# Head norms of three attention stages: squares in two float32r parts made by GpSimd, two single passes on TensorE

## The chip, the cores and the metric

The kernel runs on one core of a Trainium2 chip. The metric is the device time of one execution in microseconds, as the median of several runs. TensorE is the matrix engine, VectorE, ScalarE and GpSimd work element by element, SyncE issues the DMAs.

## The reference

Three transformer blocks over 512 tokens of width 1024, batch 1. The first has differential attention (4 heads with two maps each) beside a pooling mixer, the second sliding-window attention with sinks, the third a state-space scan (SSD, 16 heads) beside forgetting attention (16 heads); a gated feed-forward layer with a convolution follows each. In all three attentions queries and keys are normalised head by head (64 values each) before the scores:

```python
def rms_norm(x, g):
    xf = x.astype(jnp.float32)
    y = xf * lax.rsqrt(jnp.mean(xf * xf, axis=-1, keepdims=True) + EPS)
    return (y * g.astype(jnp.float32)).astype(x.dtype)

# differential attention: q, k of (B, S, 4 heads, 2, 64)
q = rms_norm(q.reshape(B, S, A_HEADS, 2, A_HEAD_DIM), q_g)
k = rms_norm(k.reshape(B, S, A_HEADS, 2, A_HEAD_DIM), k_g)
# sliding window: 16 query heads on 2 key heads; the sink is one more logit
m = jnp.maximum(jnp.max(s, axis=-1, keepdims=True), sink)
p = jnp.exp(s - m)
denom = jnp.sum(p, axis=-1, keepdims=True) + jnp.exp(sink - m)
# forgetting attention: 16 heads
qh = rms_norm_2(heads(q), q_norm_w)
kh = rms_norm_2(heads(k), k_norm_w)
```

## The kernel before

Activations lie transposed: the features on 128 partitions, the 512 tokens along a row, so that one chunk is 128x512 and holds two heads of 64. Weights come by DMA as slabs of up to 128x2048, ScalarE rounds each to float32r (w_hi) and VectorE subtracts (w_lo); a projection is three passes for each 128x128 block, w_hi with x_hi, w_hi with x_lo and w_lo with x_hi.

All engines have their own program, written out by hand in one order, and meet only by semaphores. The stages are A (differential attention), F0, C (sliding window), F1, S with the state-space scan and, at its end and after it, X (forgetting attention), and F2. Within A, C, the scan and X the projection matmuls are woven (L1178) between the small steps of the attention, in quotas that are fixed in advance, so that TensorE has work while the other engines do the softmax. In these stages step g is one block of 128 queries of two heads: scores (L862 in A, L1221 in C, L1095 in X), a woven part, the transposes of the step before (L870, L1231, L1104), then a norm job, and the values of two steps before (L881, L1246, L1117). VectorE's order in a step is finish (reciprocal of the sums and scaling of the exponentials: L1984 and L1986 in A, L2141 in C, L2503 in X), maxima (L1972, L2128, L2492), then evacuations, weight splits (L2082, 128x1024 halves) and the scaling of the next queries and keys (L1957, L2106, L2462). In A it also does the pool groups, a scan and subtractions (L2555 to L2561).

A norm job has five steps. GpSimd squares a chunk of 128x512 (L635 in A, 8 jobs; L653 in C, 10; L676 in X, 16) into a float32 tile, sq_q or sq_k by turns. TensorE multiplies with pair_ones, a float32 128x128 matrix with two blocks of 64x64 ones, which sums the squares of each head and spreads the sum over its 64 partitions (L812, L1210, L1067). ScalarE makes the inverse root by logarithm and exponential (L1419 and L1423, L1536 and L1540, L1712 and L1716), and VectorE scales the chunk. A square may overwrite its tile when TensorE has read it, which is the wait for d_stat, c_stat or f_stat. In X the queries, keys and values of a head pair come back from the scratch memory by three DMAs, for which f_in counts, and the first two jobs also wait for the last heads of the scan (y_done), whose seg and c_grow tiles lie where sq_q and sq_k do. GpSimd further multiplies C by the growing decay in the scan (L666), makes low parts of outputs (L642, L682) and sums squares for the token norms (L621).

In C the maximum of a step takes the sink in from neg_sink, and the sink's logit stands in column 256 of each probability tile (sink_columns, L2117), so that the exponential, written in place over 257 columns, adds it to the sum. There are two pairs of such tiles, used by steps in turn.

## Time and profile before

| | us |
|---|---|
| median of 3 runs | 1938.52 |
| lowest and highest | 1936.71 to 1938.80 |
| the profiled execution, its own time | 1936.25 |
| its span in the profile | 1934.4 |
| TensorE matmul busy | 1899.7 |
| VectorE busy | 1188.0 |
| ScalarE busy | 794.5 |
| GpSimd busy | 138.0 |

The span is from the first to the last instruction of the profiled execution; its own time has 1.9 us more around it. Busy times are sums of the durations of instructions; a matmul's end is modelled, so matmuls overlap in the record, and what one costs is read from start to start. In the timelines a row is one instruction or a few of the same kind: start, time from the first start to the last end, engine, line, operation and tiles, and in brackets how long the engine had stood idle before it and what released it. PE is TensorE, PEld its loading of weights, DVE VectorE, ACT ScalarE, POOL GpSimd.

By stage, A is from 0 to about 180 us, C from 565 to 740, the scan from 1190 to 1365 and X from there to 1570; the feed-forward layers lie between.

### The profile page before, as it was taken

What the parts mean: (1) busy time and instruction counts of PE and PEld (TensorE: products, weight loads), DVE (VectorE), ACT (ScalarE), POOL (GpSimd) and SP (SyncE); (2) the same over time, 40 slices, a digit from 0 to 9 for tenths busy, and PEclk for the clock granted to TensorE, in tenths of its full rate; (3) what the DMA queues carried; (4) which work ended last, traced back from release to release, by engine and by line L of the source; (5) the groups of instructions that cost most, each with busy time, mean ns of one, the idle gap of its engine ahead of it and who ended that gap; (6) DMA issues with size and microseconds to landing.
All of it is one profiled execution on the core that took longest, in us unless ns stands there. A gap on an engine that the chain in (4) does not pass through costs nothing.

```text
span 1934.4 us, 24585 instructions
## 1 busy us (share of the span) xinstructions
PE 1899.7 (98%) x9034; PEld 1504.6 (78%) x9034; DVE 1188.0 (61%) x1852; ACT 794.5 (41%) x1237; POOL 138.0 (7%) x102
## 2 busy tenths in 40 slices
PE   8999999999999999999999999999999999999999
PEld 6767888888786668888887887878666688888887
DVE  5686677356546756764476488674555667743762
ACT  4355443234435654332244433332466544422431
POOL 2011100000011001000000101111201020000000
PEclk9999999999999999999999999999999999999999
DMA  5111322322231112223322332344423122223222
GB/s 212 66 44 67 107 88 87 109 90 98 76 117 66 45 44 87 87 92 103 109 87 69 115 106 93 131 133 158 150 100 124 56 87 88 97 98 109 87 76 98
DMA packets 38304, 186.51 MB, mean 96 GB/s; under 512 B 4384, under 2 KB 4768, under 8 KB 23376
## 3 DMA queue, kind: packets, MB, share of 16 engines
q1 hardware_dynamic: 37936, 185.22, 28.3%
q8 instruction: 49, 0.80, 0.2%
q14 instruction: 31, 0.25, 0.0%
q10 hardware_dynamic: 288, 0.23, 0.0%
HBM read 176.95 MB, written 8.49 MB: 96 GB/s over the span
## 4 chain that ended last, share of the span: by engine, by line
PE 87%; DVE 7%; ACT 3%; issue 2%; DMA 0%; SPq 0%; POOL 0%; ACTq 0%; DVEq 0%; POOLq 0%
PE banks L706 54%; PE banks L1178 20%; PE banks L756 3%; DVE w_lo L1835 1%; DVE w_lo L2082 1%; PE banks L1117 1%; PE banks L1095 1%; ACT w_hi L1326 1%; PE banks L1104 1%; PE banks L1221 1%; ACT w_hi L1526 1%; DVE tmp L2211 1%; PE banks L1067 1%; PE banks L1246 1%; PE banks L1191 1%
## 5 line engine op out<-in xcount | busy, mean ns | idle before, releaser
L706 PE MATMUL banks<-xn_hi,w_hi 128*128 128x512 f32 x1240 | 486.4, 392 | 8.5 <-DVE w_lo L2584 6.0
L706 PE MATMUL banks<-xn_hi,w_lo 128*128 128x512 f32 x1240 | 483.4, 390 | 0.0
L706 PE MATMUL banks<-xn_lo,w_hi 128*128 128x512 f32 x1240 | 478.0, 390 | 0.0
L1835 DVE TENSOR_TENSOR w_lo<-raw,w_hi 128x2048 fp32r<-128x2048 f32 (+3 forms) x135 | 279.3, 2069 | 69.0 <-ACT w_hi L1326 68.5
L1326 ACT ACTIVATE w_hi<-raw 128x2048 fp32r<-128x2048 f32 (+3 forms) x135 | 229.9, 1703 | 178.0 <-PE banks L706 148.4
L706 PEld LDWEIGHTS banks<-xn_hi,w_hi 128*128 128x128 f32 x1240 | 233.4, 188 | 59.6 <-DMA con<-consts 6.0
L706 PEld LDWEIGHTS banks<-xn_lo,w_hi 128*128 128x128 f32 x1240 | 233.4, 188 | 49.8 <-issue 1.4
L706 PEld LDWEIGHTS banks<-xn_hi,w_lo 128*128 128x128 f32 x1240 | 233.4, 188 | 48.5
L1385 ACT ACTIVATE tmp<-scaled_h,par 128x512 f32<-128x512 f32 x132 | 100.5, 809 | 349.9 <-DVE scaled_h L1880 349.9
L1880 DVE TENSOR_TENSOR scaled_h<-banks,token_rs 128x512 f32<-128x512 f32 x132 | 85.0, 686 | 185.9 <-PE banks L706 165.6
L1178 PE MATMUL banks<-xn_hi,w_hi 128*128 128x512 f32 x408 | 166.1, 407 | 3.3 <-DVE w_lo L2082 3.3
L1178 PE MATMUL banks<-xn_hi,w_lo 128*128 128x512 f32 x408 | 163.1, 400 | 0.0
L1178 PE MATMUL banks<-xn_lo,w_hi 128*128 128x512 f32 x408 | 162.8, 399 | 0.0
L706 PE MATMUL banks<-hid_hi,w_hi 128*128 128x512 f32 x396 | 154.3, 390 | 1.5 <-DVE w_lo L1835 1.5
L706 PE MATMUL banks<-hid_hi,w_lo 128*128 128x512 f32 x396 | 154.1, 389 | 0.0
L706 PE MATMUL banks<-hid_lo,w_hi 128*128 128x512 f32 x396 | 154.0, 389 | 0.0
L1853 DVE TENSOR_TENSOR x<-banks,x 128x512 f32<-128x512 f32 (+1 forms) x48 | 33.2, 691 | 156.6 <-PE banks L706 137.8
L1888 DVE SCALAR_TENSOR_TENSOR tmp<-scaled_h,par,tmp 128x511 f32<-128x511 f32 x132 | 98.7, 748 | 35.4 <-ACT tmp L1385 35.4
L621 POOL TENSOR_TENSOR sq<-sq 128x512 f32<-128x512 f32 x38 | 55.9, 1470 | 873.1 <-ACT sq L1332 855.9
L2082 DVE TENSOR_TENSOR w_lo<-raw,w_hi 128x1024 fp32r<-128x1024 f32 x62 | 79.7, 1288 | 52.1 <-ACT w_hi L1526 52.1
L1892 DVE SCALAR_TENSOR_TENSOR tmp<-scaled_h,par,tmp 128x510 f32<-128x510 f32 x132 | 99.0, 750 | 14.5 <-DVE tmp L1888 12.4
L1178 PEld LDWEIGHTS banks<-xn_hi,w_hi 128*128 128x128 f32 x408 | 76.6, 188 | 30.8 <-issue 10.5
(270 smaller groups left out, 2605.2 us busy)
## 6 DMA issues: line engine op xcount, KB each, us to landing
raw<-weights SPq DMA_DIRECT2D x116, 1024.0 KB, 4.9
raw<-weights SPq DMA_DIRECT2D x24, 768.0 KB, 4.4
raw<-weights SPq DMA_DIRECT2D x24, 640.0 KB, 3.9
big<-scratch SPq DMA_DIRECT2D x40, 256.0 KB, 5.0
att<-scratch SPq DMA_DIRECT2D x16, 256.0 KB, 4.6
scratch<-stage SPq DMA_DIRECT2D x12, 256.0 KB, 4.2
scratch<-con SPq DMA_DIRECT2D x12, 256.0 KB, 2.0
out<-x SPq DMA_DIRECT2D x4, 512.0 KB, 4.0
```

The lines of the kernel that those rows point to most:

```text
L621: pool.tensor_tensor(chunk(sq, 0), chunk(sq, 0), chunk(sq, c), ALU.add).then_inc(sq_summed, 1)
L706: return pe.matmul(psum[:, 2 * p + m, :], w[:, at_:at_ + P], x_part(k), start=start, stop=stop)
L756: return pe.matmul(psum[:, 2 * (s % 2), :], w[:, at_:at_ + P], x_part(k), start=(k == 0 and t == 0), stop=(k == k_n - 1 and t == 2))
L1178: ins = pe.matmul(c_bank(u), w[:, at_:at_ + P], x_part(k), start=(k == 0 and t == 0), stop=(k == k_n - 1 and t == 2))
L1326: act.activation(w_hi[:, sl], raw[:, sl], ACT.Identity).then_inc(hi_done, 1)
L1385: act.activation(chunk(tmp, 2 * j + m), chunk(scaled_h, 2 * j + m), ACT.Identity, bias=pcol(conv_b, c), scale=pcol(conv, 3 * c + 2)).then_ ...
L1835: dve.tensor_tensor(w_lo[:, sl], raw[:, sl], w_hi[:, sl].bitcast(F32), ALU.subtract).then_inc(lo_done, 1)
L1853: last = dve.tensor_tensor(chunk(x, c), psum[:, 2 * ((a + j) % 2) + m, :], chunk(x, c), ALU.add)
L1880: dve.tensor_tensor(chunk(scaled_h, 2 * j + m), psum[:, 2 * ((a + j) % 2) + m, :], token_rs[:, :], ALU.mult).then_inc(h_scaled, 1)
L1888: me.mark(dve.scalar_tensor_tensor(out=chunk(tmp, t, 1), in0=bank[:, 0:T - 1], scalar=pcol(conv, 3 * c + 1), in1=chunk(tmp, t, 1), op0=ALU ...
L1892: dve.scalar_tensor_tensor(out=chunk(tmp, t, 2), in0=bank[:, 0:T - 2], scalar=pcol(conv, 3 * c), in1=chunk(tmp, t, 2), op0=ALU.mult, op1=A ...
L2082: ins = dve.tensor_tensor(w_lo[:, sl], raw[:, sl], w_hi[:, sl].bitcast(F32), ALU.subtract)
```

## The change

Squares and ones become float32r. A job on GpSimd is now `squares_of`: square into the float32 tile `squared`, copy that to a float32r tile (the high part), and subtract the high part from the square into a second float32r tile (the low part). Each step waits for the one before through a semaphore of GpSimd's own, pool_self, and the last for its own count. The wait for TensorE's reading stands ahead of the copy now, no longer ahead of the square. TensorE multiplies both parts with pair_ones in two accumulating products. pair_ones is a float32r tile, which VectorE copies once from the constants at the start of A (pair_ready); TensorE waits for it ahead of its first job.

The parts lie by turns in tn 1 and more 1 (jobs 0, 2, ...) and in more 2 and stage (jobs 1, 3, ...; in X more 0 instead of stage). The first job of X has its low part in mix_lo 7, so it waits for the heads up to 13 (y_done 14) and for the last input of the states (st_done 6) instead of all 16 heads; the second job waits for all 16 heads ahead of its copy.

In C the sink columns are written every second step instead of every fourth, and the wait for them stands in every second maximum.

```diff
+        def sq_parts(n, kind=""):
+            if kind == "X" and n == 0:
+                return chunk(tn_r, 1), chunk(mix_lo, 7)
+            if n % 2 == 0:
+                return chunk(tn_r, 1), chunk(more_r, 1)
+            return chunk(more_r, 2), chunk(more_r, 0) if kind == "X" else stage_r[:, :]
...
+            def squares_of(q, n, kind, read, done, freed=None):
+                hi_part, lo_part = sq_parts(n, kind)
+                me.mark(pool.tensor_tensor(squared, q, q, ALU.mult))
+                me.wait()
+                if n >= 2:
+                    pool.wait_ge(read, n - 1)
+                if freed is not None:
+                    pool.wait_ge(y_done, freed)
+                me.mark(pool.tensor_copy(hi_part, squared))
+                me.wait()
+                pool.tensor_tensor(lo_part, squared, hi_part.bitcast(F32), ALU.subtract).then_inc(done, 1)
+                pool.wait_ge(done, n + 1)
...
-                        if n >= 2:
-                            pool.wait_ge(d_stat, n - 1)
-                        q = chunk(big, 4 * which + it)
-                        pool.tensor_tensor((sq_q, sq_k)[which], q, q, ALU.mult).then_inc(d_sq, 1)
+                        squares_of(chunk(big, 4 * which + it), n, "A", d_stat, d_sq)
...
-                        if n < 2:
-                            pool.wait_ge(y_done, SSD_HEADS - 1 + n)
-                        else:
-                            pool.wait_ge(f_stat, n - 1)
-                        q = f_qkv[it % 2][which]
-                        pool.tensor_tensor((sq_q, sq_k)[which], q, q, ALU.mult).then_inc(f_sq, 1)
+                        if n == 0:
+                            pool.wait_ge(y_done, SSD_HEADS - 2)
+                            pool.wait_ge(st_done, 6)
+                        squares_of(f_qkv[it % 2][which], n, "X", f_stat, f_sq, SSD_HEADS if n == 1 else None)
...
-                pe.matmul(psum[:, 1, :], pair_ones, (sq_q, sq_k)[which], start=True, stop=True).then_inc(f_stat, 1)
+                hi_part, lo_part = sq_parts(n, "X")
+                pe.matmul(psum[:, 1, :], pair_ones, hi_part, start=True, stop=False)
+                pe.matmul(psum[:, 1, :], pair_ones, lo_part, start=False, stop=True).then_inc(f_stat, 1)
...
+                dve.wait_ge(consts_in, 16)
+                dve.tensor_copy(pair_ones, ccol("pair_ones", 0, P)).then_inc(pair_ready, 1)
...
                     it, w = g // 4, c_width(g)
-                    if g % 4 == 0:
+                    if g % 2 == 0:
                         me.wait()
...
-                    if g % 4 == 0 and 0 < g < C_STEPS:
+                    if g % 2 == 0 and 0 < g < C_STEPS:
                         sink_columns(g // 4)
```

## Rows read from the trace of the kernel before

**Rows 1.** The page, part 1: busy time, share of the span, instructions.

```profile
PE 1899.7 (98%) x9034; PEld 1504.6 (78%) x9034; DVE 1188.0 (61%) x1852; ACT 794.5 (41%) x1237; POOL 138.0 (7%) x102
```

**Rows 2.** The page, part 4: the chain that ended last, by engine.

```profile
PE 87%; DVE 7%; ACT 3%; issue 2%; DMA 0%; SPq 0%; POOL 0%; ACTq 0%; DVEq 0%; POOLq 0%
```

**Rows 3.** Timeline, X, third job: start, us, engine, line, operation, idle before.

```profile
1389.10 2.87 POOL L676 TENSOR_TENSOR tn<-big 128x512 f32<-128x512 f32 x2 [10.24 <-DMA big<-scratch]
...
1390.58 1.12 PE L1067 MATMUL banks<-tn,con 128*128 128x512 f32 x2 [0.83 <-POOL tn L676]
```

**Rows 4.** Timeline of TensorE over the first norm product of A.

```profile
39.46 0.39 PE L706 MATMUL banks<-xn_hi,w_lo 128*128 128x512 f32 x1
39.69 1.02 PE L812 MATMUL banks<-tn,con 128*128 128x512 f32 x2
40.15 0.79 PE L706 MATMUL banks<-xn_hi,w_hi 128*128 128x512 f32 x1
40.78 0.40 PE L706 MATMUL banks<-xn_lo,w_hi 128*128 128x512 f32 x1
```

**Rows 5.** By line: shortest/median/longest in ns, first and last start, shapes.

```profile
L1067 PE MATMUL banks<-tn,con x32: 592/592/697, 1366.1 to 1515.5; 128*128 128x512 f32 x32
...
L635 POOL TENSOR_TENSOR tn<-big x8: 1040/1042/1952, 30.9 to 113.2; 128x512 f32<-128x512 f32 x8
...
L682 POOL TENSOR_TENSOR mix_lo<-big,mix_hi x4: 1280/1296/1763, 1369.1 to 1377.6; 128x512 fp32r<-128x512 f32 x4
...
L2555 DVE TENSOR_TENSOR_SCAN big<-con,big x4: 1218/1222/2057, 59.8 to 105.7; 128x512 f32<-128x512 f32 x4
...
L2557 DVE TENSOR_TENSOR big<-big x4: 684/688/1332, 61.0 to 107.8; 128x510 f32<-128x510 f32 x1, 128x508 f32<-128x508 f32 x1, 128x504 f32<-128x504 f32 x1, 128x496 f32<-128x496 f32 x1
...
L2141 DVE TENSOR_SCALAR att<-att,small x64: 278/348/939, 597.4 to 709.8; 128x256 f32<-128x256 f32 x48, 128x128 f32<-128x128 f32 x16
...
L2117 DVE COPY att<-small x8: 156/159/165, 589.6 to 696.7; 128x4 f32<-128x4 f32 x8
```

**Rows 6.** Timeline of TensorE: two long stops, one in A, one in C.

```profile
88.00 0.50 PE L1178 MATMUL banks<-xn_hi,w_hi 128*128 128x512 f32 x1 [2.98 <-DVE w_lo L2082]
...
696.15 0.49 PE L1221 MATMUL banks<-att 64*128 64x128 f32 x4 [3.52 <-DVE att L2106]
```

**Rows 7.** Timeline, A: jobs 6 and 7, and TensorE's ninth transpose.

```profile
104.75 3.87 POOL L635 TENSOR_TENSOR tn<-big 128x512 f32<-128x512 f32 x2 [15.91 <-DVE big L1930]
...
111.24 0.33 PE L870 MATMUL banks<-con,att 128*128 128x128 f32 x1 [1.47 <-DVE att L1986]
```

**Rows 8.** Timeline, C: scalings of the softmax and transposes that need them.

```profile
608.79 1.20 DVE L2141 TENSOR_SCALAR att<-att,small 128x256 f32<-128x256 f32 x2
...
610.66 0.60 PE L1231 MATMUL banks<-con,att 128*128 128x128 f32 x4
...
614.58 0.53 PE L1231 MATMUL banks<-con,att 128*128 128x128 f32 x2 [0.52 <-DVE att L2141]
...
625.65 0.48 DVE L2141 TENSOR_SCALAR att<-att,small 128x128 f32<-128x128 f32 x2
...
628.14 0.38 PE L1231 MATMUL banks<-con,att 128*128 128x128 f32 x2
```

**Rows 9.** Groups by line and shape: GpSimd's smallest instruction.

```profile
L2739 POOL MEMSET const-float32-1.0<- 128x1 f32 x1 | 0.1, 98 | 0.0
```

**Rows 10.** Stretches of 1 or 2 us: busy by engine, PEclk the granted clock.

```profile
88.00:90.00 2.00, 2.00 (x9) 1.63 (x10) 1.89 (x5) 0.00 (x0) 0.85 (x1) 1.00 0.51 94
...
697.00:698.00 1.00, 1.00 (x5) 0.76 (x4) 1.00 (x5) 0.67 (x3) 0.00 (x0) 0.59 0.00 0
698.00:699.00 1.00, 1.00 (x4) 0.70 (x3) 1.00 (x2) 0.21 (x2) 0.00 (x0) 0.50 0.00 0
...
700.00:701.00 1.00, 1.00 (x10) 0.76 (x10) 0.00 (x0) 0.27 (x1) 0.00 (x0) 0.70 0.95 139
```

More of the change, by code:

```diff
@@ L185, in blocks_program @@
         con = at("con", NCON)
+        tn_at = place[0]
         tn = at("tn", 3 * T)
@@ L188, in blocks_program @@
         token_rs = at("token_rs", T)
+        more_at = place[0]
         more = at("more", 3 * T)
@@ L198, in blocks_program @@
         att = at("att", 16 * T, offset=mix_at)
+        stage_at = place[0]
         stage = [at("stage", T)[:, :], con[:, bass.ds(CONST_AT["causal"], T)]]
+        tn_r, more_r, stage_r = at("tn_r", 3 * T, F32R, offset=tn_at), at("more_r", 3 * T, F32R, offset=more_at), at("stage_r", T, F32R, offset=stage_at)
         big_r = at("big_r", 24 * T, F32R, offset=big_at)
@@ L217, in blocks_program @@
         ones = ccol("ones", 0, 128)
-        pair_ones = ccol("pair_ones", 0, 128)
+        pair_ones = at("pair_ones_r", P, F32R)[:, :]
+        pair_ready = sem("pair_ready")
         eps = ccol("eps")
@@ L223, in blocks_program @@
         bias = [chunk(att, 6), chunk(att, 7)]
-        sq_q, sq_k, sq_o = chunk(tn, 0), chunk(tn, 1), chunk(tn, 2)
+        squared, sq_o = chunk(tn, 0), chunk(tn, 2)
+        def sq_parts(n, kind=""):
[4 more added lines that the diff above has]
+            return chunk(more_r, 2), chunk(more_r, 0) if kind == "X" else stage_r[:, :]
         sub_rs = chunk(more, 0)
@@ L247, in blocks_program @@
         act_self, dve_self = sem("act_self"), sem("dve_self")
+        pool_self = sem("pool_self")
         setup_done, lam_sum, lam_exp = sem("setup_done"), sem("lam_sum"), sem("lam_exp")
@@ L613, in _ @@
         def _(pool):
+            me = Self(pool, pool_self)
+            def squares_of(q, n, kind, read, done, freed=None):
[10 more added lines that the diff above has]
+                pool.wait_ge(done, n + 1)
             def sum_squares(base):
@@ L650, in _ @@
                             pool.wait_ge(xn_ready, 24)
-                        if n >= 2:
-                            pool.wait_ge(c_stat, n - 1)
-                        pool.tensor_tensor((sq_q, sq_k)[n % 2], chunk(big, c), chunk(big, c), ALU.mult).then_inc(c_sq, 1)
+                        squares_of(chunk(big, c), n, "C", c_stat, c_sq)
                     sum_squares(24)
@@ L803, in norm_job @@
                     pe.wait_ge(d_sq, n + 1)
+                    if n == 0:
+                        pe.wait_ge(pair_ready, 1)
                     if n == 2:
@@ L811, in norm_job @@
                         pe.wait_ge(d_rs, n)
-                    pe.matmul(psum[:, bank, :], pair_ones, (sq_q, sq_k)[which], start=True, stop=True).then_inc(d_stat, 1)
+                    hi_part, lo_part = sq_parts(n)
+                    pe.matmul(psum[:, bank, :], pair_ones, hi_part, start=True, stop=False)
+                    pe.matmul(psum[:, bank, :], pair_ones, lo_part, start=False, stop=True).then_inc(d_stat, 1)
                 def turn_v(it):
@@ L1209, in norm_job @@
                         pe.wait_ge(c_rs, n)
-                    pe.matmul(psum[:, 3, :], pair_ones, (sq_q, sq_k)[n % 2], start=True, stop=True).then_inc(c_stat, 1)
+                    hi_part, lo_part = sq_parts(n)
+                    pe.matmul(psum[:, 3, :], pair_ones, hi_part, start=True, stop=False)
+                    pe.matmul(psum[:, 3, :], pair_ones, lo_part, start=False, stop=True).then_inc(c_stat, 1)
                 def scores(g):
```

## Prediction

> **What bounds the kernel now.** Three views of the page in this order: busy time by engine, the chain that ended last, and the timeline around one norm product. TensorE is busy for 98% of the span and GpSimd for 7% [rows 1]; the chain is TensorE for 87% and VectorE for 7% [rows 2]. So time taken off TensorE comes off the run, except ahead of a place where TensorE stands still for VectorE; and time put on GpSimd is free, except where TensorE or VectorE waits for it. Before the change TensorE waits for GpSimd's squares at one place, 0.83 us [rows 3]. The reader should look for those places: 88.00, 111.24, 614.58, 696.15 and 1390.58 us of the span.
>
> **What is taken away: 34 float32 products.** One head-norm product shows as two matmul records; between 39.69 and 40.78 us stand the product and one ordinary projection matmul, and an ordinary one takes 0.23 us from start to start (39.46 to 39.69) [rows 4]. The product therefore holds TensorE for 1.09 - 0.23 = 0.86 us. The X stage has 32 records, so 16 products [rows 5]; A and C have 8 and 10 by their loops, 34 in all. The change makes each into two passes over float32r tiles. The ordinary matmuls of [rows 4] have just this form (128x512, float32r), so 2 x 0.23 = 0.46 us, a saving of 0.40 us each, 34 x 0.40 = 13.6 us. This is the safest term, as the form is all over the trace; below it stands rival 4.
>
> Three of the 34 save nothing, since the stop behind them begins in another engine's chain that starts ahead of them: the fourth product of A (the stop at 88.00 [rows 6] is ScalarE's split of weights and then VectorE's), the fifth of A (the stop at 111.24 is VectorE's unbroken work [rows 7]), and the fourth of C (the stop at 614.58 [rows 8] ends a chain of ScalarE and VectorE). 3 x 0.40 = 1.2 us given back.
>
> **What is added on GpSimd.** A job was one multiplication, 1.04 us when undisturbed; now it is multiplication, copy, subtraction, each behind a wait for the one before. The subtraction reads two tiles and writes float32r as L682 does: 1.30 us [rows 5]. GpSimd makes no copy in this trace. From above it is bounded by the multiplication, 1.04 us, if the write of float32r adds nothing, from below by the smallest instruction, 0.10 us [rows 9]. L682 reads two different tiles in 1.30, the multiplication one tile twice in 1.04: the second tile costs 0.26 us, and as the copy is nearest to the multiplication I take 1.04 less that, 0.8 us (an estimate from these rows). The job is then 1.04 + 0.8 + 1.30 + 0.2 for two own waits = 3.3 us, 2.3 more than before. Where GpSimd starts more than 3.3 us ahead of TensorE, which is so for all but one of the 34 by the timelines of the two engines, the length itself is hidden. The Trainium skill, GPSIMD Engine Reference, section 4.1, says that one-input work runs on GpSimd at roughly line rate while two-input work is about twice as slow as VectorE. With its section 3.1 that makes the copy some 0.45 us, an estimate from the page; no row here shows it. By it the sum below would come out 2.1 us lower (0.35 us in six places: once in place 1, twice in place 2, three times in place 3).
>
> **Place 1, X, third job.** TensorE was already there 0.83 us before GpSimd had squared at 1389.10 us, when the last DMA had landed [rows 3]. Nothing that the change saves lies between that DMA and this product. Copy 0.8, subtraction 1.3 and two waits 0.2 come on top, and one VectorE instruction of the four splits of L2471, which GpSimd's square meets there (TensorE starts 1.48 us after its start, though it lasts 1.04), gets between, 0.6: 2.9 us more. Bounds: 1.6 (a copy of 0.1 and nothing between) and 3.7 (a copy of 1.04 and two of VectorE's between).
>
> **VectorE behind GpSimd.** The scan of L2555 takes 1.22 us, but 2.06 in one case of four, and the subtraction of L2557 0.69, but 1.33 in one of four; both exceptions [rows 5] stand beside GpSimd's two squares at 104.75 us, which took 3.87 instead of 2 x 1.04 [rows 5, 7]. Two instructions that read or write two SBUF tiles take turns and don't share. The Trainium skill, SBUF — State Buffer, in its section on the two separate sides, calls this an exclusive lock, held by the one that starts first for the whole instruction, against VectorE work with two SBUF inputs or in a two-port mode. By that rule every added GpSimd instruction can hold up VectorE once; by shared bandwidth it would stretch it by a part only. The rows above speak for the rule, and it speaks against this change. The terms that follow come from the rows.
>
> **Place 2, A, jobs 6 and 7.** They run one behind the other beside VectorE's last pool group, and the softmax that TensorE waits for at 111.24, 1.47 us [rows 7], is behind that group. There were two GpSimd instructions, now there are six. The first copy takes the turn of the former second square (0.2 shorter); the subtraction (1.3), the second multiplication (1.04) and copy (0.8) take three more turns: 2.9 us. The sixth I put behind the softmax. Bounds: 0 (VectorE's short instructions slip through) and 4.5 (all six in front, with a copy of 1.04). Jobs 5 and 8 meet VectorE too, but the transposes that need its work come microseconds later.
>
> **Place 3, C, five jobs.** From 608 us on each square meets a softmax scaling (L2141), which then takes 1.20 us for its pair [rows 8], where an undisturbed pair takes 2 x 0.3, the median of one being 0.35 from start to end [rows 5]. TensorE takes its result at 610.66, 0.7 us after it is there [rows 8]. The copy now gets between the halves: 0.8 later, and later with it the next maximum. Where a weight split follows (three of the five) TensorE is already held at the next transpose, 0.52 us at 614.58 [rows 8], and pays the 0.8: 2.4 us. In the other two the next scaling is done at 626.13 and needed at 628.14 [rows 8], 2.0 us of cover: nothing. Bounds 0 and 5 x 1.3 = 6.5. Eight more sink copies at 0.16 us [rows 5], each with a wait for it, cost 0.19 x 8 = 1.5 us of VectorE; two in eight stand where VectorE is late: 0.4 us, bounds 0 and 1.5.
>
> **The clock.** After the stop of 3.52 us that ends at 696.15 the granted clock falls from 1.00 to 0.50, 2.4 to 1.2 GHz [rows 6, 10]: four windows of 1 us from 697 us hold 0.59, 0.50, 0.50 and 0.70, so 0.41 + 0.50 + 0.50 + 0.30 = 1.7 us lost. After the stop of 2.98 us at 88.00 it stays at 1.00 [rows 6, 10]. Place 1 becomes a stop of 0.83 + 2.9 = 3.7, place 2 one of 1.47 + 2.9 = 4.4 us. Both are longer than the one that cost the clock, so I take 1.7 us twice, 3.4; bounds 0 and 3.4.
>
> **Hidden at nothing.** The copy of pair_ones on VectorE (128x128, once), placed where its constants have long been there. The new waits of squares for y_done and st_done: the first X square may start a head pair sooner; it was ready long before TensorE came to its product anyway. Its second part is written into mix_lo, the tile of the last state input, which is free by then. GpSimd's in-order queue behind the longer jobs: the splits into mix_lo come well after the squares. No DMA is added or moved.
>
> **Sum.** -13.6 + 1.2 (A and C, saved for nothing) + 2.9 (place 1) + 2.9 (place 2) + 2.4 + 0.4 (place 3) + 3.4 (clock) = -0.4 us. The profiled execution took 1936.25 us with a span of 1934.4, so it becomes 1935.9; against the median of the runs, 1938.52, it is 1938.1 us. A difference under 0.2%, 3.9 us, is called the same here, as measurements of this kernel can't tell it from none.
>
> **Rivals.** (1) GpSimd finds gaps: VectorE is not busy throughout, and if most turns fall beside nothing, only place 1 (2.9) and half of one clock fall remain: -13.6 + 1.2 + 2.9 + 0.9 = -8.6, 1929.9 us; halfway, with half of places 2 and 3 and one clock fall, 1934. For it: the 2.0 us of cover [rows 8]. Against: every C job from 608 us on met the scaling. (2) Slower, by one mechanism: the copy that rounds to float32r is slow on GpSimd. Each microsecond of it is paid once in place 1, twice in place 2 and five times in C (there the cover of 0.7 to 0.9 is used up), 8 us. From a copy of 1.35 us the kernel is slower by 4.0; at 1.5 it is -0.4 + 5.6 = +5.2, 1943.7 us. Against: VectorE and ScalarE write float32r at the pace of float32. (3) The forecast, where stops swallow the saving: between 1935 and 1942. (4) The passes are not single: two products at 0.86 instead of one, +13.6 + 13.6 - 0.4 = 1965 us; against it stand all projection rows.
>
> **Chances.** Forecast 0.42, rival 1 0.35, rival 2 0.22, rival 4 0.01. The range reaches from the full rival 1 to the 1.5 us copy of rival 2: 1930 to 1943.5; the forecast's own is 1935 to 1942. Faster by over 0.2% (rival 1 and little else) 0.36, within 0.41, slower 0.23.
>
> **What would show it.** Right or wrong step by step: the start-to-start time over a norm job (0.46 against 0.86 us); the duration of GpSimd's copy (0.8); TensorE's stop at the third X product (3.7 against 0.83) and at the ninth transpose of A (4.4 against 1.47); the pair of softmax scalings in C (2.0 against 1.20); the granted clock behind the two stops. The prediction is wrong on the fast side if VectorE's instructions keep their durations, on the slow side if the copy is over 1.35 us.

## The result and the profile after

The changed kernel takes 1943.90 us (median of 8 runs, 1942.59 to 1945.00), the kernel before 1938.65 us (8 runs beside it, 1936.71 to 1940.48). The ratio is 1.0029 with an interval of 1.0019 to 1.0039: slower by 0.29%, 5.3 us. The forecast was 1938.1 in a range of 1930.0 to 1943.5; the result lies just above its end, and on the side that had a chance of 0.23. The profiled execution took 1943.6 us, its span 1941.8.

The page of the kernel after, part 1, busy time, and part 4, the chain that ended last (they answer to [rows 1, 2]):

```profile
PE 1896.2 (98%) x9034; PEld 1509.7 (78%) x9034; DVE 1205.1 (62%) x1861; ACT 793.8 (41%) x1237; POOL 218.1 (11%) x170
...
PE 85%; DVE 8%; ACT 3%; issue 2%; POOL 1%; DMA 1%; SPq 0%; ACTq 0%; POOLq 0%; DVEq 0%
```

TensorE's busy time fell by only 3.5 us, though 13.6 us of work are gone from it: matmuls in a stretch at half the clock last longer. GpSimd has 80 us more, as meant. VectorE has 17 us more with 9 more instructions. The nine are eight sink copies of 0.16 us and the copy of pair_ones, which took 1.30 us, so most of the 17 us is in old instructions that became longer.

**The product.** TensorE over the third norm job of A, timeline (start, us, engine, line, operation, tiles):

```profile
73.11 0.39 PE L1208 MATMUL banks<-xn_lo,w_hi 128*128 128x512 f32 x1
73.34 0.39 PE L839 MATMUL banks<-tn_r,pair_ones_r 128*128 128x512 f32 x1
73.57 0.40 PE L840 MATMUL banks<-more_r,pair_ones_r 128*128 128x512 f32 x1
```

From start to start it is 0.23 us, as forecast. Where other kinds of matmul stand around the job, both forms cost more, but the difference stays: in X, from the start of the transposed mask in front to the first matmul behind, it was 0.06 + 1.01 us and is 0.03 + 0.64, which is 0.40 less. This term was right: 34 x 0.40 = 13.6 us.

**GpSimd's copy.** By source line, the two destinations of L640 (shortest/median/longest in ns, first and last start, shapes):

```profile
L640 POOL CAST tn_r<-tn x17: 609/611/2557, 31.8 to 1500.8; 128x512 fp32r<-128x512 f32 x17
L640 POOL CAST more_r<-tn x17: 609/611/1423, 38.9 to 1506.7; 128x512 fp32r<-128x512 f32 x17
```

Undisturbed the copy is 0.61 us, where I took 0.8 and the estimate worked out from the Trainium skill (GPSIMD Engine Reference, sections 4.1 and 3.1) was 0.45. Squares stayed at 1.04 and the subtraction is 1.27 to 1.31 where nothing disturbs it, as forecast.

**Place 1, X, third job** (answers to [rows 3]). Timelines of GpSimd and TensorE:

```profile
1391.24 1.60 POOL L634 TENSOR_TENSOR tn<-big 128x512 f32<-128x512 f32 x1 [10.03 <-DMA big<-scratch]
1392.91 0.95 POOL L640 CAST tn_r<-tn 128x512 fp32r<-128x512 f32 x1
1393.94 1.31 POOL L642 TENSOR_TENSOR more_r<-tn,tn_r 128x512 fp32r<-128x512 f32 x1
...
1395.31 0.50 PE L1096 MATMUL banks<-tn_r,pair_ones_r 128*128 128x512 f32 x1 [3.24 <-POOL more_r L642]
```

The stop is 3.24 us, where it was 0.83 and I forecast 3.7.

**Place 2, A** (answers to [rows 7]). What the prediction called the ninth transpose are the transposes of step 4 of A, the fifth step. GpSimd's six instructions, VectorE beside them, and TensorE:

```profile
104.82 1.89 POOL L634 TENSOR_TENSOR tn<-big 128x512 f32<-128x512 f32 x1 [15.16 <-DVE big L1962]
106.77 1.42 POOL L640 CAST more_r<-tn 128x512 fp32r<-128x512 f32 x1
108.28 1.59 POOL L642 TENSOR_TENSOR stage_r<-tn,more_r 128x512 fp32r<-128x512 f32 x1
109.95 1.07 POOL L634 TENSOR_TENSOR tn<-big 128x512 f32<-128x512 f32 x1
111.08 0.94 POOL L640 CAST tn_r<-tn 128x512 fp32r<-128x512 f32 x1
112.09 1.34 POOL L642 TENSOR_TENSOR more_r<-tn,tn_r 128x512 fp32r<-128x512 f32 x1
```
```profile
105.73 2.06 DVE L2589 TENSOR_TENSOR_SCAN big<-con,big 128x512 f32<-128x512 f32 x1
107.83 0.90 DVE L2591 TENSOR_TENSOR big<-big 128x496 f32<-128x496 f32 x1
108.65 1.25 DVE L2592 TENSOR_TENSOR big<-big,con 128x16 f32<-128x16 f32 x1
109.94 0.17 DVE L2594 TENSOR_TENSOR big<-big 128x16 f32<-128x16 f32 x1
110.03 1.52 DVE L2595 SCALAR_TENSOR_TENSOR big<-big 128x496 f32<-128x496 f32 x1
...
112.35 1.23 DVE L2018 SCALAR_TENSOR_TENSOR att<-att,small 128x128 f32<-128x128 f32 x1
...
113.64 0.48 PE L898 MATMUL banks<-con,att 128*128 128x128 f32 x1 [4.21 <-DVE att L2018]
```

The stop is 4.21 us, forecast 4.4. The line to look at is L2592: 16 columns take 1.25 us, where the same instruction took 0.16 in the kernel before (there it is L2558):

```profile
109.07 0.16 DVE L2558 TENSOR_TENSOR big<-big,con 128x16 f32<-128x16 f32 x1
```

An instruction eight times as long as before has not been stretched in proportion to its data; it stood behind GpSimd's subtraction of 108.28, which ends at 109.87. The other two turns are the last line of the pool group, L2595, behind the second square (1.52 us, 0.67 before), and L2018 of the softmax itself, behind the last subtraction (1.23 us, 0.35 before). While the second copy ran, at 111.08, VectorE's instructions had their usual lengths (L2011 at 0.17, L2013 at 0.21 us). By the rule of the Trainium skill that was weighed (SBUF — State Buffer, the section on the two separate sides: an exclusive lock for the whole instruction) this is what is to be expected, and the trace agrees: 1.25 us is the wait until 109.87 and a short rest.

**X behind the third job.** VectorE and GpSimd, and TensorE's next stop, which the forecast did not have:

```profile
1402.31 1.23 DVE L2116 TENSOR_TENSOR w_lo<-raw,w_hi 128x1024 fp32r<-128x1024 f32 x1 [4.83 <-ACT w_hi L1558]
1403.45 1.78 DVE L2496 SCALAR_TENSOR_TENSOR big<-big,small,rs 128x512 f32<-128x512 f32 x1
1405.15 0.15 DVE L2533 RECIPROCAL small<-small 128x2 f32<-128x2 f32 x1
1405.34 1.61 DVE L2537 TENSOR_SCALAR big<-big,small 128x256 f32<-128x256 f32 x2
```
```profile
1402.33 2.36 POOL L642 TENSOR_TENSOR more_r<-tn,tn_r 128x512 fp32r<-128x512 f32 x1
1404.76 1.37 POOL L634 TENSOR_TENSOR tn<-big 128x512 f32<-128x512 f32 x1
1406.19 0.61 POOL L640 CAST more_r<-tn 128x512 fp32r<-128x512 f32 x1
...
1406.33 0.44 PE L1134 MATMUL banks<-con,big 128*128 128x128 f32 x2 [1.40 <-DVE big L2537]
```

The turns can be followed: the weight split starts 0.02 us ahead of GpSimd's subtraction, which so lasts 2.36 us instead of 1.28; the scaling of the queries (L2496) waits for that, 1.78 us instead of 0.75; the square waits for the scaling; and of the scaling of the softmax (L2537) the first half waits for the square, which ends at 1406.13, and the second for the copy of 1406.19: 1.61 us for a pair that takes 0.6. TensorE stands for 1.40 us at 1406.33 and again at 1407.00 and 1407.96, 0.23 and 0.44.

**The clock.** Stretches of 1 us of the kernel after (us, busy time of PE, PEld, DVE, ACT, POOL, then the granted clock, DMA share, GB/s). Behind the stops at 86.62, 113.64 and 1395.31 and 1407:

```profile
88.00:89.00 1.00, 1.00 (x4) 0.74 (x3) 0.93 (x3) 0.00 (x0) 0.92 (x2) 0.50 0.58 229
...
115.00:116.00 1.00, 1.00 (x2) 0.43 (x2) 0.93 (x4) 1.00 (x3) 0.32 (x1) 0.50 0.00 0
...
1398.00:1399.00 1.00, 1.00 (x3) 0.72 (x3) 0.00 (x0) 0.76 (x4) 0.41 (x1) 0.50 1.01 387
...
1410.00:1411.00 1.00, 1.00 (x4) 0.27 (x4) 0.75 (x2) 0.00 (x0) 0.00 (x0) 0.50 0.93 123
...
1413.00:1414.00 1.00, 1.00 (x3) 0.78 (x3) 0.89 (x3) 1.00 (x3) 0.00 (x0) 0.50 0.99 391
```

Half the granted clock, 1.2 instead of 2.4 GHz, in four places where the kernel before had 1.00 in its profiled execution. The last two lines belong to one fall, behind the stop of 1.40 us and the two short ones that follow it; it is the longest of the four, 3.4 us lost.

**Where the time is, by stage.** Three intervals between stops of 0.63 us for weights that both kernels have (at 34.12, 508.38, 1048.58 and 1881.07 us before, 33.95, 511.16, 1051.71 and 1888.73 after). "Stops" is the sum of TensorE's waits over 0.2 us in the interval, "clock" the time lost to a granted clock of 0.5, each summed over the trace:

| | A and first feed-forward | C and second | scan, X, third |
|---|---|---|---|
| before, length | 474.26 | 540.20 | 832.49 |
| stops, clock | 7.12, 0 | 5.46, 1.7 | 7.26, 0 |
| after, length | 477.21 | 540.55 | 837.02 |
| stops, clock | 10.26, 3.4 | 8.20, 3.4 | 13.00, 5.1 |
| products saved | 3.2 | 4.0 | 6.4 |
| measured change | +2.95 | +0.35 | +4.53 |
| products, stops, clock together | +3.4 | +0.4 | +4.5 |

The three columns add up to +8.2 us against +7.8 measured, so no further cause of size is missing in these two executions. The stops grew by 11.6 us, the forecast had 9.8; the clock lost 10.2 us more, the forecast had 3.4.

### The profile page after: what moved, and what is told of

It is laid out like the page before. It is cut to its first block, busy times and chain, and to the rows that moved or that the text cites. A ratio compares the mean times of both kernels' runs of the same rounds, so it can differ in the third digit from the quotient of the medians.

```text
span 1941.8 us, 24695 instructions
## 1 busy us (share of the span) xinstructions
PE 1896.2 (98%) x9034; PEld 1509.7 (78%) x9034; DVE 1205.1 (62%) x1861; ACT 793.8 (41%) x1237; POOL 218.1 (11%) x170
## 4 chain that ended last, share of the span: by engine, by line
PE 85%; DVE 8%; ACT 3%; issue 2%; POOL 1%; DMA 1%; SPq 0%; ACTq 0%; POOLq 0%; DVEq 0%
PE banks L730 54%; PE banks L1208 19%; PE banks L780 3%; DVE w_lo L2116 1%; DVE w_lo L1867 1%; PE banks L1125 1%; PE banks L1147 1%; ACT w_hi L1358 1%; ACT w_hi L1558 1%; DVE tmp L2245 1%; PE banks L1134 1%; PE banks L1253 1%; PE banks L1278 1%; PE banks L1221 1%; DMA raw<-weights 1%
## 5 line engine op out<-in xcount | busy, mean ns | idle before, releaser
L1208 PEld LDWEIGHTS banks<-xn_hi,w_hi 128*128 128x128 f32 x408 | 77.0, 189 | 30.7 <-issue 10.2
```

Of the source, the lines that this page charges most:

```text
L1208: ins = pe.matmul(c_bank(u), w[:, at_:at_ + P], x_part(k), start=(k == 0 and t == 0), stop=(k == k_n - 1 and t == 2))
```

## The experiments

One execution can be lucky with the clock. Each run reports its mean granted clock, so for every kernel I also give the mean loss over all its executions, (1 - granted clock) x span, and the median of what is left. The clock is given to 0.001, which is 1.9 us of one execution; the means are good to about 1 us. The kernel after has 8 executions, both_sinks and a_old 6, x_nolow 4, the others 10. They ran in groups, each beside the kernel before, whose median was 1938.8 us beside x3_old to x_early, 1938.2 beside both to three_sinks, and 1939.5 beside the last four runs that are told below. A difference of medians between two groups is therefore good to about 1 us; the ratios and the rest are the better measure there.

| kernel | median us | ratio to before (interval) | clock loss | rest |
|---|---|---|---|---|
| before (80 runs in three groups) | 1938.2 to 1939.5 | 1 | 4.9 to 5.8 | 1933.4 |
| after | 1943.90 | 1.0029 (1.0019 to 1.0039) | 11.2 | 1933.0 |
| x3_old | 1938.82 | 0.9997 (0.9988 to 1.0007) | 9.5 | 1929.4 |
| before_delay | 1941.92 | 1.0014 (1.0005 to 1.0024) | 6.8 | 1935.2 |
| x_old | 1940.01 | 1.0004 (0.9994 to 1.0014) | 8.5 | 1931.5 |
| x_early | 1936.52 | 0.9988 (0.9978 to 0.9998) | 8.3 | 1928.5 |
| both | 1934.64 | 0.9980 (0.9970 to 0.9989) | 8.1 | 1926.1 |
| a67_early | 1934.38 | 0.9978 (0.9968 to 0.9988) | 7.3 | 1926.8 |
| three | 1937.03 | 0.9988 (0.9979 to 0.9998) | 7.4 | 1929.1 |
| three_sinks | 1934.65 | 0.9981 (0.9971 to 0.9990) | 7.0 | 1928.0 |
| both_sinks | 1933.82 | 0.9967 (0.9955 to 0.9979) | 8.1 | 1925.7 |
| a_old | 1934.35 | 0.9972 (0.9960 to 0.9984) | 5.8 | 1928.6 |
| x_nolow | 1930.87 | 0.9950 (0.9935 to 0.9965) | 7.2 | 1923.2 |
| before_early | 1937.52 | 0.9993 (0.9984 to 1.0003) | 4.8 | 1932.6 |

Two theories stood against each other at first. Theory 1: the loss sits in the one long stop of X and what it does to the clock. Theory 2: it is spread over all of VectorE's work that the longer GpSimd jobs hold up. Both turned out to hold a part.

**x3_old: only the third job of X in the old form.**

```diff
+        def one_product(n, kind):
+            return kind == "X" and n == 2
...
+                if one_product(n, kind):
+                    if n >= 2:
+                        pool.wait_ge(read, n - 1)
...
+                    pool.tensor_tensor(sq_whole(n), q, q, ALU.mult).then_inc(done, 1)
+                    return
...
+                if one_product(n, "X"):
+                    pe.matmul(psum[:, 1, :], pair_ones_f, sq_whole(n), start=True, stop=True).then_inc(f_stat, 1)
+                    return
```

Here `sq_whole(n)` is one float32 tile for the square, and `pair_ones_f` are the float32 ones of the kernel before.

> The changed kernel, with the third X job alone (the one whose stop is 3.24 us) in the old form: one square and one float32 product. Theory 1 (the loss in X is this one stop and what it sets off: two falls of the granted clock behind it, 3.41 + 6.83 us at half, 5.1 us lost, and the VectorE stops at 1406 to 1408 us): the stop goes back to some 0.8 us, no clock fall between 1390 and 1420 us, time 1943.9 - 2.4 - 5.1 - 1 + 0.4 = 1936 us, range 1934.5 to 1938. Theory 2 (GpSimd crowds VectorE all through X, the third job is one of sixteen): 1943.9 - 2.4 + 0.4 = 1942 us, and the clock still falls.

Measured 1938.82, 5.1 us less than after, by one job of 34; this is 0.8 us above the range of theory 1 and 3 below theory 2. The stop is back at 0.83, no granted clock of 0.5 is in X, and the third interval is 831.18 instead of 837.02 us. So it is nearer to the theory of the one stop, but that isn't all: fifteen savings would give 832.49 - 6.0 = 826.5, and of the 4.7 us over that only 1.7 are clock (a fall ahead of the scan). Some 3 us of the loss stay.

**before_delay: the kernel before, with two more GpSimd instructions ahead of the third square of X.**

```diff
+                        if n == 2:
+                            pool.tensor_tensor(chunk(more, 1), q, q, ALU.mult).then_inc(pool_self, 1)
+                            pool.wait_ge(pool_self, 1)
+                            pool.tensor_tensor(chunk(more, 2), chunk(more, 1), q, ALU.subtract).then_inc(pool_self, 1)
+                            pool.wait_ge(pool_self, 2)
                         pool.tensor_tensor((sq_q, sq_k)[which], q, q, ALU.mult).then_inc(f_sq, 1)
```

> The kernel before, with two needless GpSimd instructions (a multiplication and a subtraction, some 2.4 us together) ahead of the square of the third X job and nothing else. Theory 1: a stop of 3.2 to 3.5 us at that product, one or more clock falls behind it, 1938.65 + 2.5 + 3 to 5 = 1944 to 1946 us. Theory 2: the stop alone, 1938.65 + 2.5 = 1941 us, with no clock fall in X.

Measured 1941.92, 3.1 us over the kernel before. TensorE in its timeline, and the stretches behind:

```profile
1398.17 1.61 PE L1073 MATMUL banks<-tn,con 128*128 128x512 f32 x2 [3.67 <-POOL tn L682]
```
```profile
1399.00:1400.00 1.00, 1.00 (x3) 0.28 (x4) 0.00 (x0) 0.17 (x1) 0.12 (x1) 0.50 0.74 223
1400.00:1401.00 1.00, 1.00 (x5) 0.35 (x5) 0.03 (x1) 0.62 (x2) 0.00 (x0) 0.50 0.96 363
```

This lies between the two theories, 1941 and 1944 to 1946. Behind the stop of 3.67 us the clock fell in the profiled execution, as the prediction said, and by the 1.7 us that it said; in the mean of the ten executions the clock loss is 1.3 us more than before. The stop itself grew by 2.8 us, but the stop of 0.61 us that the kernel before has at 1400.44 is gone behind it. So the step is shown: a longer wait for GpSimd at this one place, without any other part of the change, gives a longer stop with a fall of the clock behind it. But it makes that interval only 3.8 us longer, while the changed kernel lost 4.5 us there and the 6.4 it had saved, 10.9.

**x_old: all 16 jobs of X in the old form** (`kind == "X"` in the line above).

> The changed kernel with all sixteen X jobs in the old form, A and C as changed. By the two traces X costs 4.5 us more after than before, so both theories expect 1943.9 - 4.5 = 1939.4 us. If theory 1 holds, this is slower than the kernel with only the third X job old (1936), since the other fifteen jobs save 15 x 0.40 = 6 us minus what they make VectorE late; if theory 2 holds it is faster than that one (1942).

Measured 1940.01, near the 1939.4 of both theories and slower than x3_old, as theory 1 had it. It is 3.9 us less than after: the 16 products saved in X (6.4 us) are worth less than what its jobs cost. With x3_old at 1938.82, fifteen jobs of the new form are worth 1.2 us, not 15 x 0.40 = 6.0. So 4.8 us are lost in them, apart from the third job, of which the clock loss has 1.0 (9.5 against 8.5). The intervals of the two ratios overlap, so the 1.2 is not clear of noise. The traces say the same more sharply: the third interval is 832.58 us with no clock loss in x_old and 831.18 with 1.7 in x3_old, so without the clock fifteen jobs gained 3.1 us of their 6.0.

**x_early: the third and fourth square of X start when two of the three DMAs have landed.** The values, which the third DMA brings, aren't squared. The queries' and keys' DMAs must then be known to be the first two, so SyncE waits for them before it issues that of the values.

```diff
                     sp.wait_ge(g_scaled, 8)
+                    sp.wait_ge(f_in[1], 32)
                     fetch(1, (2,))
...
-                        pool.wait_ge(f_in[it % 2], 48 * (it // 2 + 1))
+                        pool.wait_ge(f_in[it % 2], 32 if it == 1 else 48 * (it // 2 + 1))
```

> The changed kernel, with the third and fourth X job waiting for two landed transfers (queries and keys, loaded some 25 us before) instead of all three; SyncE waits for those two ahead of issuing the third, so nothing else moves. Theory 1: GpSimd has both parts ready before TensorE comes, no stop, no clock fall in X: 1943.9 - 3.2 - 5.1 - 1 = 1934.5 us, range 1933 to 1936. Theory 2: the stop of 3.2 us goes, VectorE stays crowded and the clock falls all the same: 1940.5 us.

Measured 1936.52, 7.4 us less than after, with every job in the new form, and near theory 1 (0.5 us above its range). The third interval is 829.01 us, 8.0 less than after and 3.5 less than before. The timelines of GpSimd and TensorE:

```profile
1379.79 1.06 POOL L635 TENSOR_TENSOR tn<-big 128x512 f32<-128x512 f32 x1
1380.91 0.61 POOL L641 CAST tn_r<-tn 128x512 fp32r<-128x512 f32 x1
1381.60 2.16 POOL L643 TENSOR_TENSOR more_r<-tn,tn_r 128x512 fp32r<-128x512 f32 x1
...
1391.49 0.47 PE L1097 MATMUL banks<-tn_r,pair_ones_r 128*128 128x512 f32 x1
```

The parts are there 7.7 us before TensorE comes. So it was not the length of the new job that made the stop here, but that the job waited for a transfer that it does not need. Nine stops for VectorE are left in X, 5.4 us in sum, where the kernel before has four, 2.3 us.

**both: x_early, and the seventh square of A waits for the fifth finish of the softmax.**

```diff
+                        if n == 6:
+                            pool.wait_ge(d_fin, 5)
                         squares_of(chunk(big, 4 * which + it), n, "A", d_stat, d_sq)
```

> The X squares of the second head pair start early, as in x_early (1936.5), and the seventh square of A waits for the fifth finish of the softmax, so that it no longer runs between VectorE's last pool group and that softmax. Theory 1 (stops are made by GpSimd's place, not its length): TensorE's stop near 113 us falls from 4.2 to about 1.5 us, the clock fall behind it (1.7 us lost) goes: 1936.5 - 2.7 - 1.7 = about 1932. Theory 2 (the lost time of A only moves, as the seventh square is then late itself): the stop comes back at the product of that job, 1935.5 to 1937.

Measured 1934.64, between the two theories. The stop fell from 4.25 to 2.48 us, not to 1.5: GpSimd's first three instructions still stand in the pool group, with the same 1.25 us for 16 columns. The clock loss hardly moved (8.3 to 8.1 us), so the 1.7 us for the clock were wrong: in the profiled execution of both it is behind the other stop, near 88 us, that the clock fell. The rest gained 2.4 us.

**a67_early: x_early, and jobs 6 and 7 of A in the old form** (`kind == "A" and n in (5, 6)`).

> As x_early, but jobs 6 and 7 of A are one float32 square and one float32 product again. Theory 1 (the six GpSimd instructions are what held VectorE): stop near 113 us back at 1.5 us, -2.7 for the stop, -1.7 for the clock, +0.8 for two float32 products: about 1933. Theory 2 (the stop there comes from the order of VectorE's own work, as the kernel before had 1.47 us too): the stop stays over 3 us, 1936 to 1938.

Measured 1934.38: the stop is 1.83 us, so the six GpSimd instructions are what had lengthened it. The rest is 1.7 us less than in x_early, and the clock loss 1.0 less, where 1.7 was expected.

**three: both, and each square of C from the sixth on waits for TensorE's product of the job before.**

```diff
+                        if n >= 5:
+                            pool.wait_ge(c_stat, n)
                         squares_of(chunk(big, c), n, "C", c_stat, c_sq)
```

> As both, and each square of C from the sixth on waits for TensorE's product of the job before it, which puts it away from the scaling of the softmax. Theory 1 (taking turns with the scalings costs C about 2 us): stops in C back to those of before, C and the layer after it 540.5 - 2 = 538.5 us, in all 1930. Theory 2 (in C the chain of the maxima and scalings is the bound whatever GpSimd does): C stays within 0.5 us, in all as both, 1932.

A miss: 1937.03, 2.4 us over both. The C interval is 541.37 us instead of 539.39. VectorE and GpSimd in C:

```profile
618.42 1.30 POOL L635 TENSOR_TENSOR tn<-big 128x512 f32<-128x512 f32 x1 [17.23 <-PE banks L1247]
...
618.94 1.61 DVE L2180 TENSOR_SCALAR att<-att,small 128x256 f32<-128x256 f32 x2
...
622.22 0.44 PE L1283 MATMUL banks<-att 128*64 128x128 f32 x4 [1.17 <-DVE big_r L2184]
```

The pair of scalings at 611 us is down to 0.61 us, and the transposes' stop from 0.93 to 0.33; but the later square meets the next pair, which is now the one of 1.61 us, and TensorE stands 1.17 instead of 0.33 us one step on, and as long again near 650 and 679 us. This place within the step is no better, and another was not tried: a collision that is moved is not gone.

**three_sinks: three, with the sink columns every fourth step again.** That leaves the contents of the tiles as in the kernel before, and no part of the result out.

```diff
-                    if g % 2 == 0:
+                    if g % 4 == 0:
                         me.wait()
...
-                    if g % 2 == 0 and 0 < g < C_STEPS:
+                    if g % 4 == 0 and 0 < g < C_STEPS:
                         sink_columns(g // 4)
```

> As three, with the sink columns written every fourth step as in the kernel before (which steps' columns are rewritten changes nothing in the probabilities). Theory 1, the forecast's term: eight more small copies with waits cost 0.4 us, so 0.4 faster than three. Theory 2: their place in VectorE's order, ahead of a maximum, costs more, 1.5 us.

1934.65, and the C interval 0.80 us shorter (540.57 against 541.37). The rest of the 2.4 us between the medians is not in a place of the profile that I can name.

**both_sinks: both, with the sink columns every fourth step again**, the best of the kernels that compute everything.

> As both (1934.6), with the sink columns written every fourth step as in the kernel before. Theory 1 (the added copies stand ahead of maxima and finishes on which TensorE waits: three against three_sinks gave 0.8 us in C): 1933.8 us, C and the layer after it 0.4 to 0.8 us shorter than in both (539.4). Theory 2 (only hidden work of VectorE): 1934.6, C the same.

1933.82, 0.9967 of the kernel before. The C interval is 538.59, again 0.80 us shorter than in both: the sink copies cost 0.8 us, twice the forecast's 0.4, within its bounds.

**a_old: x_early, with all eight jobs of A in the old form.**

> As x_early (1936.5), but all eight jobs of A are one float32 square and one product again. Theory 1 (A saves nothing: eight products, 3.2 us, against 2.8 us of the stop near 113 and 0.4 of the stop near 87, and the clock falls more often): both stops back at 1.5 and 2.98 us, A no slower than in x_early, in all 1934 to 1935. Theory 2 (the products of A do pay, the clock is as it was): 0.4 to 1 us slower than x_early, 1937.

1934.35 us, 2.2 less than x_early. Its stops in A, in TensorE's timeline:

```profile
88.30 0.79 PE L1230 MATMUL banks<-xn_hi,w_hi 128*128 128x512 f32 x1 [2.97 <-DVE w_lo L2141]
...
114.18 0.33 PE L917 MATMUL banks<-con,att 128*128 128x128 f32 x1 [1.48 <-DVE att L2043]
```

The rest is the same as in x_early (1928.6 and 1928.5), the clock loss 5.8 instead of 8.3 us. So in A the change gives just what it takes, 3.2 us against two longer stops, and costs some 2.5 us of clock in the mean (6 executions against 10).

**x_nolow: both, where X has no low part from the fifth job on.** GpSimd makes a copy of 128x1 in place of the subtraction, and both products take the high part, so the sums of squares lack the low parts.

```diff
-                pool.tensor_tensor(lo_part, squared, hi_part.bitcast(F32), ALU.subtract).then_inc(done, 1)
+                if kind == "X" and n >= 4:
+                    pool.tensor_copy(small[:, 159:160], squared[:, 0:1]).then_inc(done, 1)
+                else:
+                    pool.tensor_tensor(lo_part, squared, hi_part.bitcast(F32), ALU.subtract).then_inc(done, 1)
...
+                if n >= 4:
+                    lo_part = hi_part
```

> As both (1934.6), but in X from the fifth job on the low part is left out: in place of the subtraction GpSimd makes a copy of 128x1, and both products take the high part, so that TensorE's work stays the same. Theory 1 (the GpSimd instructions of a job take turns with VectorE's and make it late; the subtraction is the longest): the stops in X fall from 5.2 us in sum to that of the kernel before, 2.3: 1932. Theory 2 (VectorE is late since TensorE is faster by 6.4 us there and comes to its waits sooner): the stops stay, 1934.6.

1930.87, 3.8 us less than both, with TensorE's work unchanged. VectorE beside the fifth job of X, first in both, which has the low part, then in x_nolow:

```profile
1401.03 1.94 DVE L2540 TENSOR_SCALAR big<-big,small 128x384 f32<-128x384 f32 x2
...
1402.33 1.22 DVE L2124 TENSOR_TENSOR w_lo<-raw,w_hi 128x1024 fp32r<-128x1024 f32 x1
1403.47 1.52 DVE L2504 SCALAR_TENSOR_TENSOR big<-big,par,rsk 128x512 f32<-128x512 f32 x1
...
1405.11 0.90 DVE L2545 TENSOR_SCALAR big<-big,small 128x384 f32<-128x384 f32 x2
```

The pair of softmax scalings (L2540 in both, L2545 in x_nolow) takes 0.90 us instead of 1.94. The stops for VectorE in X fall from nine with 5.4 us to five with 2.8 us, near the 2.3 us of the kernel before. The other theory, that VectorE is late only since TensorE is faster, can explain no more than the small part that is left: TensorE has the same work here.

**before_early: the kernel before, with x_early's edit.**

> The kernel before, with X's third square starting when two of three DMAs have landed, as in x_early. Theory 1 (what x_early gained for the kernel before is the stop of 0.83 us and no more): 1937.8. Theory 2 (the early start lets VectorE's work move too, as x_early lost 8 us against after in this stage): 1935 or less, and then the change itself is worth nothing beside it.

1937.52, and the third interval 1.0 us shorter (831.53 against 832.49). By this interval the early start is worth 1.0 us to the old form and 8.0 to the new one. So the change itself, put where it does not wait, is worth 1937.5 - 1934.6 = 2.9 us (both; 2.5 by the ratios, as the two are of different groups), and without the sink copies 3.7 (both_sinks; 5.0 by the ratios), of the 13.6 that it takes off TensorE.

## Why the prediction was wrong, point by point

Every term that the sum had was right in its direction. The sum failed by one step that was put at nothing, X behind the third job, and by one that was too small, the clock. In the order of the prediction:

- **The 34 products, -13.6 us: right.** 0.40 us each, seen in all three stages. Rival 4 is out. Its price was summed wrongly: two products of 0.86 us instead of one cost 34 x 0.86 = 29.2 us more, where the forecast has 13.6 less, so it would have been 1981 us and not 1965; nothing else hangs on it.
- **The copy, 0.8 us: too dear, 0.61.** This ends rival 2: the kernel is slower, but not by a slow copy.
- **Place 1, +2.9: right in kind, 2.4.** The copy took 0.95 here, 0.61 where nothing disturbs it, and the square 1.60, with VectorE's turn in it. before_delay and x_early show it from both sides.
- **Place 2 and what A saves for nothing, +3.7 in all: 3.1** (7.12 to 10.26 us of stops), of which 0.4 stands at 86.62 us, where the stop grew from 2.98 to 3.37 by just the product that was saved. Place 2 itself is 2.7 against 2.9, and that is partly luck: of the three turns forecast the subtraction and the second square took theirs (1.1 and 0.9 us more on VectorE), the second copy none, and the last subtraction, which I had put behind the softmax, took one of 0.9 in it.
- **Place 3, C, and its sink copies, +3.2 with the fourth product: 2.7** (5.46 to 8.20). Inside it the sink copies were 0.8, not 0.4. The first copy of the new form did get between the halves of a scaling: the pair at 611.01 us takes 1.61 us, where I forecast 2.0 and it was 1.20 [rows 8]. The answering line of the kernel after, VectorE's timeline:

```profile
611.01 1.61 DVE L2175 TENSOR_SCALAR att<-att,small 128x256 f32<-128x256 f32 x2
```

- **X behind the third job, put at nothing: 3.3 us. The first failed step.** "Where GpSimd starts more than 3.3 us ahead of TensorE ... the length itself is hidden" is true of the product and false of VectorE. I had looked for collisions with VectorE in A and C, and in X only at the one job. The stops of the third interval that were over 0.2 us, without the third job's, went from 6.4 to 9.8 us, all of the growth in X. x_old, x3_old and x_nolow show it by leaving the work out; x_nolow's 2.9 us of rest is nearly all of it. What it was: each added GpSimd instruction can hold up VectorE in X too, and TensorE then waits for VectorE.
- **The clock, +3.4: some 6 us. The second failed step, a mis-sized term.** The mean loss over the executions went from 5.3 to 11.2 us. Of the 5.8 (before rounding), about 2.9 go with the stops of X (after to x_early) and 2.5 with those of A (x_early to a_old), each where 1.7 was forecast; some 0.5 is left for C, within what the means are good for. The forecast took one clock fall for each long stop, from one execution. It missed that stops which are already there cost the clock in some executions, and more often once they are longer: in the profiled execution before, the clock had held after 2.98 us [rows 6, 10], and in after, with 3.37 us at the same place, it fell.
- **Hidden at nothing:** the copy of pair_ones and the new waits of the first squares cost nothing that the profile shows.

Sum with the sizes found: -13.6 + 11.6 (stops) + 5.8 (clock) = +3.8 us, against +5.3 between the medians. The 1.5 us between is not explained; it is about what the clock means are good for. The stops are of one execution each. Against the forecast's -0.4: stops +1.8 (X +2.8, A and C together -1.0), clock +2.4, and the 1.5 that is not explained.

The forecast's last warning, wrong "on the slow side if the copy is over 1.35 us", named the wrong cause for the right side. None of the rivals was the true one: the result is slower by the clock and by VectorE in X, not by the copy. That the chance given to a slower result was 0.23 is no credit to the forecast, as it stood on the copy.

What stays open is which of A's two stops costs its 2.5 us of clock. both has the shorter second stop and lost as much as x_early; a_old has both stops shorter and lost less. A kernel with only the fourth job of A in the old form was not tried.

## What to carry to other kernels

Moving work from a full engine to an idle one is paid for at every neighbour of the idle one: list all instructions of VectorE that stand beside the new GpSimd work in every stage, not only in those where TensorE waits already. Then ask of each wait in front of the moved work whether it is for data that this work reads: here one wait for an unneeded transfer turned a gain of 2 us into a loss of 5. And a saving on TensorE in front of a stop only lengthens that stop, and the clock can then be lost on top: in A the longer stops took back all of the 3.2 us saved, and the clock some 2.5 more.

## What the runs showed of the hardware

**After a stop of one and the same length the clock fell in some executions and not in others, and more often after longer stops.** The 14 profiled executions, one of each kernel, have these stops of TensorE, and around their end a fall of the granted clock to 0.5 or none:

| place | stop, us | clock fell |
|---|---|---|
| X, third job | 0 to 0.83 | 0 of 12 |
| X, 1406 us, kernel after, with 0.23 and 0.44 us more within 1.7 us | 1.40 | 1 of 1 |
| A, near 21 us | 1.27 to 2.29 | 3 of 14 (at 1.86, 2.05 and 2.29, not at 1.88 and 1.91) |
| A, fifth step | 1.46 to 1.83 | 0 of 5 |
| before the scan, 1172 to 1178 us | 2.3 | 5 of 14 |
| A, fifth step | 2.48 to 2.50 | 4 of 5 |
| A, near 88 us | 2.97 to 2.98 | 2 of 4 |
| A, near 88 us | 3.37 | 9 of 10 |
| C, near 697 us | 3.5 | 14 of 14 |
| X, third job | 3.24 and 3.67 | 2 of 2 |
| A, fifth step | 4.2 to 4.3 | 4 of 4 |

One fall cost 1.7 or 3.4 us. So a trace of one execution can't say that a stop of 2.98 us is safe; two of four say otherwise. What decides between two equal stops, no run here shows, and part of the difference between the rows may be the place and not the length. A forecast would have to take a share of a fall for each stop of some 2 us and more, those that are already there included, as the kernel before already loses some 5 us in the mean and not the 1.7 of its profiled execution in front of its end.

**A tiny VectorE instruction can wait a whole GpSimd instruction.** 16 columns took 1.25 us beside a subtraction of 1.59 (0.16 in the kernel before). In the timelines of place 2 and behind the third job of X, between two GpSimd instructions that follow each other through a semaphore, a waiting VectorE instruction got its turn each time, and between two of VectorE's own a GpSimd one did; no engine was starved.

**GpSimd at 128x512:** multiplication of one tile with itself 1.04 us, copy to float32r 0.61, subtraction of two tiles into float32r 1.27 to 1.31. The copy with its one input costs 0.61, not the 0.8 worked out from the other two.
